# First-layer attentions in slots behind the projection and output steps, output stage in two halves, modulation groups moved

## The reference

```
n = rms_norm(x);  proj = n @ w_in                 # 45 column tiles of 128
g_qkv = silu(short_conv(proj[gla part]))          # 16 tiles: q, k, v
gla_out = gated linear attention(4 heads, chunks of 64, decay from gate_lr)  * silu(out_gate)
nsa_out = g0 * compressed + g1 * selected + g2 * window attention   (8 heads, 2 key/value heads)
h = x + concat(gla_out, nsa_out) @ w_out          # GLA is rows 0..1023 of w_out, NSA rows 1024..2047
x = h + (silu(rms_norm(h) @ w_gate) * (rms_norm(h) @ w_up)) @ w_down
# second model: modulation (c, c_ctx) @ mod_w gives shift, scale and gate of its two layers
x = x + gate * rms_norm(attention(...) @ w_out);  x = x + gate * rms_norm(pooling(...) @ w_out)
```

## Time and profile before

| | us |
|---|---|
| median of 3 runs | 2238.25 (2237.99 to 2240.48) |
| the profiled execution | 2238.62 |
| its span | 2236.9, mean TensorE clock 0.944 |
| TensorE matmul busy | 2108.6 (94%) |
| VectorE busy | 1571.8 (70%) |
| ScalarE busy | 885.7 (40%) |
| GpSimd busy | 168.8 (8%) |

### The profile page before, as it was taken

One profiled execution on the slowest core, in us unless ns is written; L12 is line 12 of the kernel. 1 busy time (PEld: TensorE's weight loads), 2 busy tenths in 40 slices (PEclk: granted clock), 3 DMA queues, 4 the chain that ended last, 5 costly groups with the idle time before them and its releaser, 6 DMA issues.

```text
span 2236.9 us, 43074 instructions
## 1 busy us (share of the span) xinstructions
PE 2108.6 (94%) x16344; PEld 2049.5 (92%) x16344; DVE 1571.8 (70%) x2046; ACT 885.7 (40%) x1170; POOL 168.8 (8%) x268
## 2 busy tenths in 40 slices
PE   7999978389999999999999999899999998899997
PEld 7999977368999999999999999899889997899997
DVE  7787463556877778677666768776777876777655
ACT  5343331244443333333333345424545343444442
POOL 0000000001200000000000001100000021000011
PEclk9999966569999999999999999999999998999998
DMA  6588510005867768677687866556445885458662
GB/s 233 184 263 259 178 61 32 0 0 176 275 209 233 227 223 300 205 226 226 221 275 256 274 195 218 176 170 204 145 142 171 265 270 178 133 187 270 209 192 98
DMA packets 119552, 434.07 MB, mean 194 GB/s; under 512 B 13216, under 2 KB 13600, under 8 KB 119216
## 3 DMA queue, kind: packets, MB, share of 16 engines
q1 hardware_dynamic: 90672, 328.11, 45.6%
q0 software_dynamic: 28800, 104.87, 14.0%
HBM read 430.83 MB, written 2.10 MB: 194 GB/s over the span
## 4 chain that ended last, share of the span: by engine, by line
PE 87%; DVE 8%; ACT 2%; issue 1%; DMA 1%; POOL 0%; SPq 0%; POOLq 0%; ACTq 0%; DVEq 0%
PE ps L502 25%; PE ps L503 25%; PE ps L504 25%; PE ps L572 2%; PE ps L567 2%; DVE w_lo L1249 1%; PE ps L853 1%; PE ps L863 1%; PE ps L610 1%; DMA raw<-w_main 1%; PE ps L741 1%; ACT w_hi L943 0%; DVE sq L1325 0%; PE ps L578 0%; PE ps L743 0%
## 5 line engine op out<-in xcount | busy, mean ns | idle before, releaser
L943 ACT ACTIVATE w_hi<-raw 128x1024 fp32r<-128x1024 f32 x610 | 634.0, 1056 | 663.9 <-PE ps L504 637.0
L502 PE MATMUL ps<-a_hi,w_hi 128*128 128x256 f32 x3024 | 860.6, 285 | 7.5 <-DVE a_lo L1335 5.7
L503 PE MATMUL ps<-a_lo,w_hi 128*128 128x256 f32 x3024 | 857.8, 284 | 0.0
L504 PE MATMUL ps<-a_hi,w_lo 128*128 128x256 f32 x3024 | 857.6, 284 | 0.0
L1249 DVE TENSOR_TENSOR w_lo<-raw,w_hi 128x1024 fp32r<-128x1024 f32 x610 | 741.5, 1257 | 103.3 <-ACT w_hi L943 102.2
L502 PEld LDWEIGHTS ps<-a_hi,w_hi 128*128 128x128 f32 x3024 | 582.4, 193 | 10.9 <-issue 6.7
L503 PEld LDWEIGHTS ps<-a_lo,w_hi 128*128 128x128 f32 x3024 | 582.8, 193 | 0.0
L504 PEld LDWEIGHTS ps<-a_hi,w_lo 128*128 128x128 f32 x3024 | 582.6, 193 | 0.0
L502 PE MATMUL ps<-b_hi,w_hi 128*128 128x256 f32 x1920 | 553.2, 288 | 10.3 <-DVE b_lo L1654 4.9
L503 PE MATMUL ps<-b_lo,w_hi 128*128 128x256 f32 x1920 | 546.6, 285 | 0.0
L504 PE MATMUL ps<-b_hi,w_lo 128*128 128x256 f32 x1920 | 546.5, 285 | 0.0
(11 more groups left out here) (287 smaller groups left out, 1367.5 us busy)
## 6 DMA issues: line engine op xcount, KB each, us to landing
raw<-w_main SPq DMA_DIRECT2D x610, 512.0 KB, 4.4
side<-w_side POOLq DMA_DIRECT2D x200, 512.0 KB, 4.5
x_tok<-x_in SPq DMA_DIRECT2D x4, 512.0 KB, 6.4
ctx_tok<-ctx_tok SPq DMA_DIRECT2D x1, 2048.0 KB, 11.9
y_out<-o_tok SPq DMA_DIRECT2D x4, 512.0 KB, 2.8
table<-counts_tab SPq DMA_DIRECT2D x1, 512.0 KB, 13.5
cons<-cons_in SPq DMA_DIRECT2D x1, 478.0 KB, 10.3
table<-masks_in SPq DMA_DIRECT2D x1, 448.0 KB, 10.1
```

What stands on the lines that cost most here:

```text
L502: pe.matmul(out_ap, wh, act_hi[:, kt, :], start=first and n == 0, stop=False)
L503: pe.matmul(out_ap, wh, act_lo[:, kt, :], start=False, stop=False)
L504: mm = pe.matmul(out_ap, wl, act_hi[:, kt, :], start=False, stop=last and n == len(blocks) - 1)
L943: act.activation(w_hi[:, slot, :], raw[:, slot, :], ACT.Copy).then_inc(hi_ready, 1)
```

## The change

The first layer becomes 61 steps with a chain of its own, `l1_chain()`, on TensorE, ScalarE and VectorE. The column tiles come in a new order: the gate tile (`last`), the convolved tiles, the out gate, NSA keys and values, NSA queries. The softplus, scan and levels of GLA run in slots 2 to 23, its outputs in 24 to 37, the compression in 28 to 39, NSA head h in slots 40 + h to 44 + h. The output stage is split: `outg` (8 steps) multiplies the GLA half of `w_out`, two output tiles a step, and `outn` (8 steps) the NSA half; the first runs while the NSA chain still does. The layer's squares are added on GpSimd in pairs of tiles. The six levels' loop, masks and products are as before; NSA works on one head for both query halves instead of eight heads of one half. Buffers move: most attention tiles now lie in `B`, `PR` and the side area, because `A` holds the activations until the last projection. GpSimd clears `g_keep`, `g_q`, `g_k` at the start instead of VectorE. `w_main` keeps its layout in memory; the first 61 steps' halves are addressed through `stored_half`.

Modulation: no group stays in the first layer; `up2` is cut into `up2` and `up2b`, `ev_q` into `ev_q` and `ev_q2`, one group each; `down1` takes a group with two vectors. The sum of the `ev_out` group is taken after the normalisation that follows that stage. On GpSimd, in stages with both, the square is added before the next side load is issued.

```diff
-STAGES = [("conv", 16), ("rest", 29), ("out", 16),
-          ("up0", 32), ("down0", 16), ("up1", 32), ("down1", 16), ("up2", 24), ("down2", 16),
-          ("ev_kv", 8), ("ev_q", 16), ("ev_z", 16), ("ev_out", 16),
+STAGES = [("last", 1), ("conv", 16), ("gout", 8), ("nkv", 12), ("nq", 8), ("outg", 8), ("outn", 8),
+          ("up0", 32), ("down0", 16), ("up1", 32), ("down1", 16), ("up2", 12), ("up2b", 12), ("down2", 16),
+          ("ev_kv", 8), ("ev_q", 8), ("ev_q2", 8), ("ev_z", 16), ("ev_out", 16),
...
-MOD_GROUPS = {"rest": 0, "out": 4, "up0": 1, "down0": 2, "up1": 3, "down1": 5, "up2": 6,
-              "ev_kv": 7, "ev_q": 8, "ev_z": 9, "ev_out": 10, "od_z": 11}
+MOD_GROUPS = {"up0": 0, "down0": 1, "up1": 2, "down1": 3, "up2": 4, "up2b": 5,
+              "ev_kv": 6, "ev_q": 7, "ev_q2": 8, "ev_z": 9, "ev_out": 10, "od_z": 11}
...
+    return range(DT * k // n, DT * (k + 1) // n)      # products of step k of a stage with n steps
...
+LV_T = (10, 13, 16, 18, 20, 22)
+PAIR_T = 39
+HEAD_T = 40
...
 # TensorE, slot t of l1_chain (excerpt)
+                    if t in LV_T:
+                        lv = LV_T.index(t)
+                        pe.wait_ge(S("g_mul"), 2 * (lv + 1))
+                        pe.wait_ge(S("g_msk"), 2 * (lv + 1))
+                        gla_scores(lambda h: g_q[:, h, :], lambda h: g_k[:, h, :])
+                    if t == 11:
+                        pe.wait_ge(S("g_kdr"), 1)
...
+                    h = nsa_head(t, 3)
+                    if h is not None:
+                        pe.wait_ge(S("at_pt"), h + 1)
+                        if h:
+                            pe.wait_ge(S("at_out"), h)
...
+                        for part in range(2):
+                            pe.matmul(out, v_nsa[:, 0, 2 * part + g, :], pt_first[:, b, part, :], start=part == 0, stop=False,
+                        pe.matmul(out, v_cmp[:, g, :], pt_cmp[:, b, :], start=False, stop=False, skip_group_check=True)
+                        for part in range(2):
+                            mm = pe.matmul(ps[:, 7, P:T], v_nsa[:, 1, 2 * part + g, :], pt_second[:, b, part, :],
...
+                    h = nsa_head(t, 0)
...
+                        for tt in range(TT):
+                            keys = (tt + 1) * P
+                            mm = pe.matmul(ps[:, 2 + tt, 0:2 * keys], pr[:, NQ + h, tt * P:(tt + 1) * P],
+                                           pr[:, k0:k0 + 3:2, 0:keys], start=True, stop=True)
...
+            def run_out(stage, tile0):
+                for k in range(COUNT[stage]):
+                    s = FIRST[stage] + k
+                    pe.wait_ge(dve_read, s - 1)
+                    for c in range(2):
+                        pe.wait_ge(lo_ready, 2 * s + c + 1)
+                        half_products(ps[:, s % 2, c * T:(c + 1) * T], c, s % 2, range(8), b_hi, b_lo, tile0, True, True)\
+                            .then_inc(halves_used, 1)
+                    next(chain)
+
+            chain = l1_chain()
+            run("last", (a_hi, a_lo), split=[("x_lo", 0)], chain=chain)
+            for stage in ("conv", "gout", "nkv", "nq"):
+                run(stage, (a_hi, a_lo), chain=chain)
+            pe.wait_ge(S("g_out"), 4)
+            run_out("outg", 0)
+            pe.wait_ge(S("at_out"), 8)
+            run_out("outn", 8)
...
 # ScalarE, slot t: heads (excerpt)
+                    h = nsa_head(t, 1)
+                        act.wait_ge(S("at_nb"), h + 1)
+                        for tt in range(TT):
+                            for part in range(2):
+                                ins = act.activation((prob0, prob1)[tt][:, h % 2, part, :], ..., ACT.Exp, ...)
+                    h = nsa_head(t, 3)
+                        act.activation(pt_first[:, b, :, 0:P], ..., ACT.Copy)
+                        act.activation(pt_cmp[:, b, :], ps[0:N_CMP, 4, T:2 * T], ACT.Copy)
+                        act.activation(pt_first[:, b, :, P:T], ..., ACT.Copy)
+                        act.activation(pt_second[:, b, :, :], ..., ACT.Copy).then_inc(S("at_pt"), 1)
+                    j = nsa_pair(t, 1)
+                        act.activation(q_rs[:, :, 2 * j:2 * j + 2], q_rs[:, :, 2 * j:2 * j + 2], ACT.Sqrt)
...
 # TensorE and VectorE, after ev_out
             norm("od")
+            sum_mods("ev_out")
...
             norm("od", res, sq, lambda f: od_gain[:, f:f + 1], lambda f: mods[:, 48 + f, 0:1], a_hi, a_lo)
+            read_mods("ev_out")
```

More of the change, by code:

```diff
@@ L75, with products @@
 assert len(MOD_STAGES) == MOD_TILES // 8
-def mods_a_step(stage):
-    return DT // min(DT, COUNT[stage])
-MOD_BANK = {"ev_kv": 4, "ev_q": 6}
+def products(stage, k):
+    if stage not in MOD_GROUPS:
+        return ()
+    n = COUNT[stage]
+    if stage in SECOND:
+        return (k // 2,) if k % 2 else ()
+    return range(DT * k // n, DT * (k + 1) // n)
+MOD_BANK = {"ev_kv": 4, "ev_q": 6, "ev_q2": 6}
 BOTH = (0, 1, 2, 3)
-CMP_AT = DT
+CMP_AT = 0
 SIDE_HALVES = 2 * CMP_HALVES + 2 * MOD_TILES
@@ L361, in build @@
         silu_ready = S("silu_ready")
[L364 to L377, removed]
         def v_ev(src, tt, f):
@@ L418, in loads @@
                     pair(0, s1 - 1, 1)
+            for h in range(4, 2 * FIRST_LAYER):
+                load(0, h, stored_half(h // 2, h % 2))
             for stage, count in STAGES:
+                if FIRST[stage] < FIRST_LAYER:
+                    continue
                 loads(stage)
@@ L543, in run @@
                     norm_sums(summed)
-                if stage in MOD_GROUPS:
+                if stage in MOD_GROUPS and stage != "ev_out":
                     sum_mods(stage)
@@ L880, in _ @@
             run("ev_q", (b_hi, b_lo), chain=chain)
+            run("ev_q2", (b_hi, b_lo), chain=chain)
             run_z("ev_z", 0, (b_hi, b_lo), chain=chain)
@@ L1120, in ctx_chain @@
+            for stage in ("last", "conv", "gout", "nkv", "nq", "outg", "outn"):
+                ahead(stage, chain=chain)
+            ffn_tiles(7)
             def ctx_chain():
@@ L1202, in _ @@
             ahead("ev_q", chain=chain)
+            ahead("ev_q2", chain=chain)
             ahead("ev_z", extra=z_silu_steps(act, "ev_z", 0), chain=chain)
@@ L1275, in read_mods, with reading @@
                                   vbc(col("mod_b", t0, 8), vecs), ALU.add).then_inc(S("mods_read"), 1)
-            def reading(stage, read, first=0, splits=(), between=None, chain=None, after=None):
-                each = mods_a_step(stage) if stage in MOD_GROUPS else 0
+            def reading(stage, read, first=0, chain=None, after=None):
                 def body(i, k):
@@ L1286, in body @@
                         next(chain)
[L1287 to L1292 removed]
+                    if isinstance(i, int) or k < DT:
+                        for m in products(stage, k):
+                            add_mod(stage, i, m)
                     if read is not None:
@@ L1658, in add_res @@
+            chain = l1_chain()
+            reading("last", scaled_read(LAST), chain=chain)
+            reading("conv", conv_read, chain=chain)
+            reading("gout", scaled_read(GOUT), chain=chain)
+            reading("nkv", scaled_read(NKC), chain=chain)
+            reading("nq", scaled_read(NQ), chain=chain)
             def add_res(i, k, bank):
```

1191 lines of the change are left out of this document (659 added, 532 removed).

## The result

The changed kernel takes 2112.45 us (median of 4 runs, 2107.82 to 2116.58), the kernel before 2238.12 beside it: a ratio of 0.943 (95% interval 0.942 to 0.945), 125.7 us less. The profiled execution took 2116.58 us with a span of 2114.7.

The account below looks back on a forecast made before the run. TensorE was taken as the bound outside the first layer's attentions. First layer 2.9 + 349.8 + 93.4 + 10 = 456.1 for 592.4 us; 2238.62 - 136.3 + 8.8 = 2111 us, own range 2100 to 2124.

Parts of the forecast that it names:

- What bounds, and what can be saved: First layer: TensorE bounds elsewhere; only the attentions' 231.8 us, less TensorE's own work there, can be saved.
- TensorE's load in the slots: First-layer slots: attention products priced at full clock, 89.2 us, plus 4.2 for 38 slots with work: 93.4 us.
- Stalls: First-layer slots: TensorE waiting for VectorE and ScalarE, 4 us in conv slots, 0 in gout/nkv, 6 in NSA: 10.
- Table loads: NSA slots: one ScalarE table switch each, 1.28 us without further drain; the skill's drain would add some 4 us.
- Sum +8.8: Stages after the first layer: moved modulation sums, waits, up2, ev_q and ev_out together cost 8.8 us more.
- The 1 us for up2's load: up2: 16 products in 12 steps, VectorE at 5.2 of 5.73 us a step, transfers at 305 GB/s: 1 us.
- rival D: up2 starves for weights if 275 GB/s is its limit, 153 us for 138: 2126 us; chance 0.07.
- The -3.4 of ev_out: End of ev_out: its modulation sum moves behind the normalisation, so VectorE's rstd no longer waits for it: -3.4 us.
- A: First-layer slots: the other engines' chain is longer than TensorE's part, NSA slots 2.5 us longer: 2147 us; chance 0.20.
- B: First-layer slots: VectorE's slot work starts only when the step has ended: 2335 us; chance 0.04 together with E.
- C: Whole kernel: nothing stalls (-10 us) and stage ends are free (-6): 2095 us; chance 0.09.
- E: First layer: the moved work does not overlap at all but costs no more: 2247 us; chance 0.04 together with B.

Follow-up runs that it names:

- half compression: Changed kernel with every second of the eight narrow products of each compression half left out: 2108.21 us beside 2111.8.
- two extra kernels: Changed kernel with one, then two, added VectorE operations ahead of the slot's work in slots 41 to 51: 2119.05 and 2127.89 us.
- second control: The changed kernel run again without edits, beside its two neighbours: 2111.8 us (2105.79 to 2115.38).
- swapped order: Changed kernel with VectorE's first-layer slot put behind its wait for the step's products: 2243.64 us, ratio 1.0014 to the kernel before.
- best: Changed kernel with 64-column sums in feed-forward stages, products up to a step earlier, up2 and up2b products over eleven of twelve steps: 2089.97 us.

## Why the prediction came out right, step by step

The forecast of 2111.0 is 1.45 us under the median, but part of that is luck. The profiled execution, 2116.58, is 5.6 above it: the first layer came out 2.5 better than forecast, the rest 6.6 worse, and the first weights are multiplied 1.3 later (22.18 for 20.91). The median is 4.1 under the profiled execution, in which the clock's dips were deep.

**What bounds, and what can be saved: right.** The 231.8 us of the attentions of the earlier trace rows were turned into TensorE work beside full-clock steps. `up0` begins at 475.75, forecast 477; clock 1.00 in the slots, forecast over 0.9. The half compression shows that TensorE's own queue is the bound in slots 28 to 35.

**TensorE's load in the slots: near.** 453.6 - 2.9 - 349.8 - 4.1 of waits leaves 96.8 for the 93.4 charged, 4% more. In the NSA slot the weight step (5.84), the transposes (0.79) and the compressed scores (0.81 for 0.84) are as priced; scores are 1.38 for 1.28 and values 2.13 for 1.78. Of the values, four of 256 columns take 0.96 and two with 15 rows 0.62, so 0.24 and 0.31 each, where I had taken 0.216 from the earlier trace rows.

**Stalls: the sum was 10, the trace shows 4.1.** The softplus and scan slots show at most 0.3, a wait for `w_lo` at 77.92 (charged 1.1), the levels 0.4 (0.6), the product `g_kd` 1.5 (2.1). NSA: 1.9 of waits for the 6 charged; but a full slot is 10.95 long, which is about my 10.5 + 0.5. The half microsecond was there, as work of TensorE and not as a wait. The two extra kernels bear out "close enough to charge": 0.65 to 0.8 us more on the chain and it would have set the time.

**Table loads: the row was right.** A load of 1.28 us at 353.74, the square root at 355.03, and the load at 361.05 ends 0.19 before the exponential, which waited 0.18 of it for `at_nb`. The Trainium skill (ScalarE: Activation LUTs, "What ACT_TABLE_LOAD costs") has a further drain of about 1.38 us for each switch; this trace, as that of the earlier trace rows, shows none, and the 4 us are not there.

**The later part: the failed step.** In "Sum +8.8" a term is missing: the later part came to +15.4, and what the runs show in its place is the low clock behind the modulation sums. The three further sums and the barrier at slot 16 are in the rows (`ev_q` +3.0 for 3.2 charged). The waits rose by 2.4, from 4.6 to 7.0, for the 4.6 charged. The 1 us for up2's load does not show, and no matmul waits for `raw` there (rival D), with 307 GB/s moved around `up2`'s sum. What was missing is the clock behind the sums: in the kernel before three dips (behind the sums at 799.80, 901.42 and 1095.25) cost 3.4, 5.1 and 1.7 = 10.2 us by the same count, in the changed one six cost 20.5. With 5.1 of sums, 2.4 of waits, 1.3 of barrier, 10.2 of clock and the 3.3 gained at `ev_out` the sum is 15.7 for 15.4 measured. I had written that the clock needs no term of its own; that holds for the first layer alone, and only as long as its slots have spare time. How large the term comes out differs from execution to execution: in the second control's profile the dips cost 10.2 us. The row was there to be read: the earlier trace rows has the low clock in a stretch of narrow matmuls, and I used it to price them and did not ask what follows behind one. With neither waits nor one-column sums the clock stays at 1.00 at all six and the time falls by 22 us.

**The -3.4 of ev_out: right here, but priced at half clock.** The gain is in the trace (3.3), and its place too: 5.57 us from the last square to `rstd` became 2.26. But I had taken a duration at half clock for the price of the instructions. At the full clock the same sum costs this path 1.5 us, of which 0.45 is left at the next norm.

**Rivals.** A is out as the bound, though only by 0.65 to 0.8 us a slot. B is out here and confirmed as a danger: swapped order costs all of the gain, though less than B said. C's first half (no stalls) was half right; its second, free stage ends, needs the edits of best, and then the time is below C's 2095. D and E are out.

## What to carry to other kernels

A serial part put in slots behind a streamed step is worth what TensorE idles in it, less its own matmuls at the full clock, but only if the other engines' slot work is issued ahead of their wait for that step. Read the granted clock in the 10 us behind every short wait or burst of narrow matmuls at a stage's end: here such an end cost up to 5 us that no wait shows, and finishing the other engine's work one step earlier and widening the narrow products to 64 columns gave 22 us for a handful of changed lines. Before counting a duration of the trace as saved, see at which clock it was taken.

## What the hardware showed that I had not expected

- TensorE's granted clock falls while the engine is busy without a gap, behind a wait of 1 to 2 us with a burst of 32 one-column matmuls: in the changed kernel's profile to 0.50 over 6 us behind the sums at 761.63 and 955.52. It also fell (0.72) behind such a burst with no wait, and behind a wait of 1.45 us with a 64-column burst of 16 (0.74 and 0.90). The single-vector sums without a wait in the second model (five of them, at 1393.5 to 1976.3) leave it at 1.00; around the sixth, at 1780.12, it is 0.84 and then 0.54, but that one stands behind a norm in which TensorE was idle and the clock 0.50 (1766 to 1770).
- The same end of a stage falls to different depths in different executions: behind `up2`'s sum 0.63 and 0.69 in one and 1.00 in another.
- A matmul of 64 columns costs a sum next to nothing over one of one column: 1.90 us for 16 against 1.84 in the timelines, 3.68 for 32 against 3.63.
- A sum of sixteen one-column matmuls takes 3.41 us at a clock of 0.50 and 1.84 at 1.00, so its price in a trace depends on what the engine did before it.
